# One large gate projection ahead of the level products, and a new order of work between the last mixer half and the first expert

## What is computed

```python
h = rmsnorm(x, g_pre_mix) * (1.0 + sc_mix) + sh_mix
proj = h @ w_in                                   # u | q k v | z | a | b
pool_out, _ = pool_mixer(u, pool_buf, start_pos, w_pool, pool_scale)
qkv_c, _ = causal_conv(qkv, conv_buf, conv_w)
o, s_new = gated_delta_rule(q, k, v, g, beta, s0)  # solves (I + L) T = I per chunk
o = o * rsqrt(mean(o * o) + EPS) * gdn_norm_w * silu(z)
x = x + gt_mix * rmsnorm(concat([pool_out, o]) @ w_out, g_post_mix)
h = rmsnorm(x, g_pre_ffn) * (1.0 + sc_ffn) + sh_ffn
logits = h @ router_w + router_b                  # 32 experts, top 4, softmax gates
f = sum over the 4 chosen experts e of gate_e * ((up_e + 1) * glu_e) @ w_down[e] + b_down[e]
x = x + gt_ffn * rmsnorm(f, g_post_ffn)
```

## Time and profile before

| | us |
|---|---|
| runs, median (lowest to highest, 3 runs) | 1219.59 (1217.38 to 1220.33) |
| the profiled execution's own time | 1221.47 |
| its span | 1219.5 |
| TensorE matmul busy | 1032.8 (85%) |
| VectorE busy | 396.7 (33%) |
| ScalarE busy | 168.6 (14%) |
| GpSimd busy | 125.7 (10%) |
| moved by DMA | 463.68 MB, 380 GB/s in the mean |

### The profile page before, as it was taken

The page is one execution under the profiler, slowest core; times in us unless marked ns, Lnnn a source line. Parts: engine busy times, 40 slices in busy tenths (PEclk is TensorE's granted clock), DMA queues, the critical chain, the costliest instruction groups (busy, mean ns, idle before and its releaser), DMA issues.

```text
span 1219.5 us, 31937 instructions
## 1 busy us (share of the span) xinstructions
PE 1032.8 (85%) x11996; PEld 503.7 (41%) x11997; DVE 396.7 (33%) x1155; ACT 168.6 (14%) x459; POOL 125.7 (10%) x325
## 2 busy tenths in 40 slices
PE   4899997997899869899779999898856799999864
PEld 4678775646333314333223334333311233334321
DVE  1044594765323213133113332332211223223313
ACT  2252313133000000010001001001000000001002
POOL 0042003100111001001101110100100000000100
PEclk9898998997999989999889999999988899999997
DMA  9945936989899999999999997999999999999996
GB/s 338 337 144 207 328 131 185 343 298 389 360 426 427 429 429 429 427 429 427 429 429 428 427 429 301 430 430 427 428 428 428 430 430 427 428 428 428 430 430 280
DMA packets 77831, 463.68 MB, mean 380 GB/s; under 512 B 11531, under 2 KB 31185, under 8 KB 53146
## 3 DMA queue, kind: packets, MB, share of 16 engines
q1 hardware_dynamic: 70479, 460.88, 92.1%
q10 hardware_dynamic: 7315, 2.27, 0.9%
HBM read 455.56 MB, written 7.57 MB: 380 GB/s over the span
## 4 chain that ended last, share of the span: by engine, by line
PE 62%; DMA 18%; DVE 9%; SPq 4%; issue 4%; ACT 1%; DVEq 1%; ACTq 0%; POOLq 0%; POOL 0%
PE psum L663 26%; PE psum L682 14%; DMA weights<-in_w_gu 11%; PE psum L638 4%; PE psum L1027 4%; DMA work<-in_w_down 4%; SPq L914 2%; PE psum L615 2%; PE psum L1278 2%; PE psum L632 2%; DMA weights<-in_w_ada 2%; PE psum L1032 1%; DVE work L2404 1%; DVE work L2048 1%; DVE work L2409 1%
## 5 line engine op out<-in xcount | busy, mean ns | idle before, releaser
L663 PE MATMUL psum<-weights,work 128*32 128x512 f32 x2928 | 346.6, 613 | 89.4 <-DMA weights<-in_w_gu 45.1
L663 PEld LDWEIGHTS psum<-weights,work 128*32 128x32 f32 x2928 | 92.8, 111 | 311.7 <-issue 240.2
L682 PE MATMUL psum<-weights,work 128*32 128x256 f32 x2624 | 162.3, 398 | 35.4 <-DVE work L2418 32.1
L2404 DVE STREAM_TRANSPOSE work<-psum 128x256 f32<-128x256 f32 x53 | 23.9, 450 | 425.8 <-PE psum L663 425.8
L682 PEld LDWEIGHTS psum<-weights,work 128*32 128x32 f32 x2624 | 84.5, 114 | 107.8 <-issue 58.3
L1824 ACT ACTIVATE work<-work x53 | 22.1, 416 | 505.6 <-DVE work L2408 505.6
L615 PE MATMUL psum<-work 128*32 128x257 f32 (+3 forms) x1296 | 88.9, 387 | 1.1 <-ACT work L1771 1.1
L2428 DVE STREAM_TRANSPOSE work<-work 128x288 f32<-128x288 f32 x53 | 25.3, 478 | 191.8 <-PE psum L638 191.8
L1027 PE MATMUL psum<-work,weights 128*128 128x288 f32 x320 | 81.0, 410 | 0.0
L663 PE MATMUL psum<-work 128*32 128x512 f32 x464 | 60.0, 637 | 8.9 <-DMA work<-in_w_gu 8.9
L1027 PEld LDWEIGHTS psum<-work,weights 128*128 128x128 f32 x320 | 59.8, 190 | 17.5 <-issue 1.8
(11 more groups left out here) (405 smaller groups left out, 933.6 us busy)
## 6 DMA issues: line engine op xcount, KB each, us to landing
weights<-in_w_gu SPq DMA_DIRECT2D x112, 2048.0 KB, 35.7
weights<-in_w_down SPq DMA_DIRECT2D x48, 2048.0 KB, 38.1
work<-in_w_gu SPq DMA_DIRECT2D x16, 2048.0 KB, 32.4
work<-in_w_down SPq DMA_DIRECT2D x16, 2048.0 KB, 42.6
weights<-in_w_ada SPq DMA_DIRECT2D x12, 2048.0 KB, 12.6
weights<-in_w_in SPq DMA_DIRECT2D x6, 2048.0 KB, 13.4
weights<-in_w_out SPq DMA_DIRECT2D x2, 2048.0 KB, 8.3
out<-weights SPq DMA_DIRECT2D x8, 512.0 KB, 10.1
```

The costliest lines, as they stand in the source:

```text
L663: last = mm(bank(GB)[SLOTS * n:SLOTS * n + SLOTS, :].rearrange("p (a x) -> p a x", a=4), xTm[:, k, :], gu[:, k % 2, n], start=k == 0, stop ...
L682: last = mm(bank(YB)[SLOTS * q:SLOTS * q + SLOTS, 0:QW], hT[:, k, :], dn[:, k % 4, QW * q:QW * q + QW], start=k == 0, stop=k == KT - 1)
L2404: v.transpose(features, of_slots[0]).then_inc(s["hid_step"], 1)
```

## The change

There are two parts. **In the front part** the work after unit 23 moves behind unit 24, and that after unit 24 behind unit 25, on TensorE and ScalarE alike; the last transposes of values come ahead of the last level's updates. On SP the eight small stores of modulated gates and the load of the sequence mask go ahead of the store of solved blocks; the sample states are loaded right behind the blocks, and the gate rows (`gate_rows`) after them.

**Between the last mixer half and the first expert** `normed` writes the whole scaled chunk, and TensorE transposes it with its transpose operation; the last state products stand inside the last mixer half (5 of its 8 matmuls, then the state, then 3); the third chunk is transposed and brought back ahead of other work; gates are normalized on VectorE ahead of the ranks, VectorE sets the first gate column in GpSimd's place, one gather takes all 257 columns after the gate's transposes, and the products with zeros are gone (the bias products start the accumulators). On SP the stores and loads of the second expert are reordered.

The core of the diff (ScalarE's units move as TensorE's do, its `rows_back` as TensorE's `back`; bank numbers are left out):

```diff
-        diag = [X3.at(2 * GW + P * c, P) for c in range(3)]
+        xt = [M.at(6400, D), M.at(3072, D), mix_s]
...
+                    if first and c == 2:
+                        pe.wait_ge(s["h2"], 3)
...
-            pe.wait_ge(s["h2"], 3)
-            pe.wait_ge(s["rank_done"], 2)
-            gather_by(sel_first, QW).then_inc(s["router_ps"], 1)
+                    mm(samples_out[r, :], gT[r, span(2)], b_down_sb[r, :], start=True, stop=False)
+
+            pe.wait_ge(s["h2"], 2)
+            pe.wait_ge(s["rank_done"], 1)
             for r in range(NQ):
                 for q in range(NQ):
                     rows, to = slice(SLOTS * r, SLOTS * r + SLOTS), slice(SLOTS * q, SLOTS * q + SLOTS)
-                    last = mm(bank(GB)[to, 2 * NE * r:2 * NE * (r + 1)], ident[:, rows], rank[:, 0:2, :].rearrange("p c e -> p (c e)"),
+                    last = mm(bank(RB)[to, 2 * NE * r:2 * NE * (r + 1)], ident[:, rows], rank[:, 0:2, :].rearrange("p c e -> p (c e)"),
                               start=True, stop=True)
             last.then_inc(s["router_ps"], 1)
-            pe.wait_ge(s["selT"], 1)
-            for half in range(2):
-                for q in range(NQ):
-                    r = slice(NE * q, NE * q + NE)
-                    mm(total(q, half), selT[r, 0:P], consts_sb[r, 0:QW], start=half == 0, stop=False)
-            mm(samples_out, selT[0:NE, 0:P], consts_sb[0:NE, 0:QW], start=True, stop=False)
-            pe.wait_ge(s["cum"], 4)
-            of_first = bounds(0)
             pe.wait_ge(s["gate_done"], 1)
             for c in range(3):
                 for q in range(NQ):
-                    last = mm(bank(YB)[NE * q:NE * q + NE, AT[c]:AT[c] + ROWS[c]], gate[0:ROWS[c], c, :],
+                    last = mm(bank(TB)[NE * q:NE * q + NE, AT[c]:AT[c] + ROWS[c]], gate[0:ROWS[c], c, :],
                               ident[0:ROWS[c], 0:ROWS[c]], start=True, stop=True)
             last.then_inc(s["router_ps"], 1)
+            pe.wait_ge(s["rank_done"], 2)
             pe.wait_ge(s["cur_set"], 2)
-            pe.wait_ge(s["xTm"], 1)
-            for c in range(3):
-                for g in range(NQ):
-                    r = slice(SLOTS * g, SLOTS * g + SLOTS)
-                    last = mm(bank(XB)[r, QW:GC], sel_first[r, c, :] if c == 2 else sel_first[:, c, :],
-                              h2s[r, QW:GC] if c == 2 else h2[:, c, g, QW:GC], start=c == 0, stop=c == 2)
-            last.then_inc(s["xg_ps"], 1)
-            pe.wait_ge(s["gbT"], 1)
-            pe.wait_ge(s["rank_b"], 1)
+            gather_by(sel_first, GC, True).then_inc(s["xg_ps"], 1)
+            pe.wait_ge(s["cum"], 4)
+            of_first = bounds(0)
             expert(0, 0, of_first)
             for r in range(1, PERIOD):
                 expert(0, r)
...
             sp.dma_start(w_out_sb[1], w_out_half(1)).then_inc(s["wout_in"], 16)
+            sp.wait_ge(s["modG"], 4)
+            for j in range(4):
+                sp.dma_start(gm_dram[:, :, P * j:P * j + P], modG[32 * j:32 * j + SEQS]).then_inc(s["side_st"], 16)
+            sp.wait_ge(s["slot_used"], used("in", 5))
+            sp.dma_start(seqmask, cc("seqmask").rearrange("p (b t) -> p b t", b=NSEQ)).then_inc(s["seq_in"], 16)
+            for j in range(4):
+                sp.dma_start(gs_dram[:, j // 2, :, j % 2].rearrange("t b c -> b t c"), modG[32 * j + 1:32 * j + SEQS, 2:4]
+                             ).then_inc(s["side_st"], 16)
             sp.wait_ge(s["pooled"], 2)
             sp.wait_ge(s["t0"], 2)
             sp.dma_start(t_dram.rearrange("c h r k i j -> (c h r) (k i j)"), blk_tu[0:BLOCKS]).then_inc(s["blk"], 16)
             t_block_loads(sp, 0)
-            sp.wait_ge(s["modG"], 4)
-            for j in range(4):
-                sp.dma_start(gm_dram[:, :, P * j:P * j + P], modG[32 * j:32 * j + SEQS]).then_inc(s["modG_st"], 16)
-            sp.wait_ge(s["slot_used"], used("in", 5))
-            sp.dma_start(seqmask, cc("seqmask").rearrange("p (b t) -> p b t", b=NSEQ)).then_inc(s["seq_in"], 16)
-            for j in range(4):
-                sp.dma_start(gs_dram[:, j // 2, :, j % 2].rearrange("t b c -> b t c"), modG[32 * j + 1:32 * j + SEQS, 2:4]
-                             ).then_inc(s["modG_st"], 16)
-            sp.wait_ge(s["modG_st"], 128)
-            gate_rows(sp, 0, gm_tok, "gm_in")
+            sp.wait_ge(s["side_st"], 128)
             sp.wait_ge(s["pool_ps"], 2)
             sp.wait_ge(s["s_silu"], 3)
             sp.wait_ge(s["norm_ps"], 2)
...
                 sp.dma_start(Ssm[:, :, b], state_ssm[0, b].rearrange("h k v -> k h v")).then_inc(s["ssm_in"], 16)
+            gate_rows(sp, 0, gm_tok, "gm_in")
...
             sp.wait_ge(s["mix_ps"], 3)
             load(1, 0)
             store_states(1)
+            store_states(2)
+            sp.wait_ge(s["mix_ps"], 4)
+            load(1, 1)
             sp.wait_ge(s["ssm_out"], 16 * 5)
             load(1, 2)
-            sp.wait_ge(s["mix_ps"], 4)
-            load(1, 1)
             for q in range(NQ):
                 sp.dma_start(bgu_rows[NE * q:NE * q + NE], b_gu[0].rearrange("e (a n x) -> n e a x", a=4, n=NQ)[q]
                              ).then_inc(s["bgu_in"], 16)
+            store_x1(2)
+            load(1, 4)
+            sp.wait_ge(s["x2T_ps"], 3)
             for q in range(NQ):
                 sp.dma_start(b_down_sb[NE * q:NE * q + NE, :], b_down[0][:, QW * q:QW * q + QW]).then_inc(s["rb_in"], 16)
-            store_states(2)
-            store_x1(2)
+            sp.wait_ge(s["side_st"], 128 + 32)
+            load(1, 3)
             sp.wait_ge(s["x2T_ps"], 5)
-            load(1, 4)
-            sp.wait_ge(s["ssm_out"], 16 * (1 + H))
-            load(1, 3)
...
-                if u == 23:
+                if u == 24:
                     pe.wait_ge(s["qkdT"], 3)
                     pe.wait_ge(s["blk"], 16 * BLK_LOADED)
                     level_product(pe, mm, 1)
                     conv_tails()
                     level_updates(pe, mm, 1)
                     level_updates(pe, mm, 2)
-                if u == 24:
+                if u == 25:
                     pe.wait_ge(s["kv_tok"], 4)
                     to_tokens(4, PB)
                     level_product(pe, mm, 3)
                     level_product(pe, mm, 4)
                     last_tails()
-                    level_updates(pe, mm, 3)
-                    level_updates(pe, mm, 4)
-                if u == 25:
                     pe.wait_ge(s["s_silu"], 3)
                     pe.wait_ge(s["kv_tok"], 5)
                     to_tokens(5, PB)
+                    level_updates(pe, mm, 3)
+                    level_updates(pe, mm, 4)
 
...
-                    last = mm(out, x_sb[0:n, c, P * k:P * k + P], diag[c][0:n, 0:n], start=True, stop=True)
+                    last = tr(out, xt[c][0:n, P * k:P * k + P], ident[0:n, 0:n])
...
             state_update(1, 1)
             pe.wait_ge(s["ssq"], 5)
             state_update(2, 0)
-            mix_half(1, 4, 1).then_inc(s["mix_ps"], 1)
+            mix_half(1, 4, 1, 0, 5)
+            state_update(2, 1)
+            mix_half(1, 4, 1, 5).then_inc(s["mix_ps"], 1)
             transposes_x2(0, 6)
-            state_update(2, 1)
-            pe.wait_ge(s["s_new"], 2 * H)
+            pe.wait_ge(s["s_new"], 2 * H - 2)
             transposes_x2(1, 1)
             logit_parts(0, 6, 7)
+            transposes_x2(2, 4)
+            logit_sums(0, 7)
             sample_logits(1)
-            logit_sums(0, 7)
-            transposes_x2(2, 4)
             pe.wait_ge(s["lg_sb"], 2)
             back(0, 6)
             pe.wait_ge(s["lg_sb"], 3)
+            pe.wait_ge(s["s_new"], 2 * H)
             logit_parts(2, 1, 2)
+            back(2, 4)
+            logit_sums(2, 2)
             earlier_ranks()
-            logit_sums(2, 2)
+            last_ranks()
             pe.wait_ge(s["h2"], 1)
             back(1, 6)
-            last_ranks()
-            back(2, 4)
-            pe.wait_ge(s["h2"], 2)
...
-                ts(diag[c][0:n, 0:n], ident[0:n, 0:n], st[0:n, 4 + c:5 + c], None, ALU.mult).then_inc(s["xn2"], 1)
+                ts(xt[c][0:n, :], x_sb[0:n, c, :], st[0:n, 4 + c:5 + c], None, ALU.mult).then_inc(s["xn2"], 1)
...
-            for t in range(2):
-                new_states(2, 0, t)
+            for m in range(2):
+                for t in range(2):
+                    new_states(2, m, t)
             add_mix(2)
-            for t in range(2):
-                new_states(2, 1, t)
             normed(2)
             v.wait_ge(s["x2T_ps"], 3)
             v.wait_ge(s["modT"], 4)
...
+            v.wait_ge(s["gate_done"], 1)
+            ts(gate_col[:, 0:2 * NQ].rearrange("p (c g) -> p c g", c=2), gate[:, 0:2, 0:1].to_broadcast([P, 2, NQ]),
+               1.0 / ALPHA, None, ALU.mult).then_inc(s["cur_set"], 1)
+            ts(gate_col[:, 2 * NQ:], gate[:, 2, 0:1], 1.0 / ALPHA, None, ALU.mult).then_inc(s["cur_set"], 1)
...
-            v.wait_ge(s["router_ps"], 7)
```

(14 more changed lines are left out.)

61 lines of the change are left out of this document (28 added, 33 removed).

## The result

The changed kernel takes 1211.47 us (median of 5 runs, 1205.39 to 1212.91), the kernel before 1218.16 us beside it (5 runs, 1217.38 to 1220.33): a ratio of 0.9925, with a 95% interval of 0.9905 to 0.9945. It is faster, as forecast, but by 6.7 us in place of 17.3, and outside the range of 1199.5 to 1208.5. The profiled execution took 1211.84 us (span 1210.1).

A forecast was written before the change was run, and what follows sets the result against it. The DMA stream of expert weights was taken as the bound, TensorE only around the dip at 738 to 754 us. Gains of 10.0 + 5.0 + 2.3 = 17.3 us gave 1219.59 - 17.3 = 1202.3 us, range 1199.5 to 1208.5.

The forecast's parts named there:

- (1): Before the level products: unit 24 fills TensorE's 7.16 us wait for solved blocks; gain 7.1 us.
- (3): Products from L1245 on no longer wait for a copy on ScalarE; gain 1.4 us.
- Term (4): Level products: unit 25 and six transposes cover VectorE and ScalarE putting results back; price 0, up to 1.5 us otherwise.
- Term (5): SP's front order: early small stores, sample states issued from about 188.3 us, and later gate rows all cost 0.
- Term (2): Level products: without idle time TensorE's clock stays at 2.4 GHz; gain 1.5 us, bounds 0 and 2.5.
- Term (6): Front: state loads closely following the last block pieces delay those pieces by 0, at most 1.9 us.
- Term (7): Before the first expert: an earlier first reload removes DMA's pause at 305 to 314 us; gain 5.0 us.
- Term (8): Router stretch: earlier stores of the last states fill DMA's idle time; gain 2.3 us, bounds 1 and 2.5.
- A: Last mixer half to first expert: TensorE at half clock, a DMA pause stays; 1203.3 to 1207.3 us, chance 0.14.
- B: Level products: steps wait for VectorE and ScalarE, or sample states come late; 1206.7 us, chance 0.14.
- C: Front: blocks land later, so the large projection does not fill the wait; 1210 to 1211 us, chance 0.05.
- D: TensorE-bound stretch up to 768 us: held at 1.2 GHz, the kernel gets slower; 1223.3 us with 42 us, chance 0.02.

The follow-up runs named there:

- e11: Changed kernel with sample states loaded head by head: two heads behind the block pieces, four behind the last projection unit, then gate rows; 1206.35 us, ratio 0.9888.
- e7: Changed kernel with gate rows issued first, then all sample states head by head behind the last projection unit; 1206.41 us, ratio 0.9888.
- e8: Changed kernel with products by a scaled diagonal in place of VectorE's scaling and TensorE's transposes; 1210.84 us, ratio 0.9916.
- e1: Kernel before with only the front part of the change; 1214.07 us, ratio 0.9972.
- e12: Kernel before with only the front part, states by head: two behind the block pieces, four behind the last projection unit; 1209.35 us, ratio 0.9934.
- e2: Changed kernel without the front part of the change; 1213.86 us, ratio 0.9958.
- e3: Changed kernel, but SP waits for the last projection unit before issuing the eight state loads; 1213.10 us, ratio 0.9961.

## Why the prediction was right and wrong

**The bound** was read rightly. From 314 us on the stream of DMA runs at 428 GB/s in every trace, and its lead at 100 MB is kept up to the dip: against the second trace of before it is 4.9 us in the changed kernel at 100 MB and 4.8 at 240 MB, and 11.6 and 11.5 in e11.

**Terms (1) and (3)** held: no wait for the blocks (7.16 us before), none in front of L1245's successor (1.38 before). **Term (4)** held at 0.

**Term (5) is the step that failed.** It let the states' loads start earlier "as far as the products that need them" and priced them at 0. Nothing in that sentence asks what else is on DMA at that moment. **Term (2)** held where it was read and was undone by the stop: from the first level products to the next unit TensorE needs 3.1 us (189.38 - 186.28) in place of 5.0, 1.9 won for 1.5 reckoned, but behind the stop more was lost again at 1.2 GHz. The price is the difference of the stretches in the changed kernel and e11, 52.9 - 45.4 = 7.5 us: 3.0 for the stop (3.54 less 0.58), and 4.5 for the work behind it, from the transposes to the first products for the states (11.3 us in place of 6.8). Without it (e11) the stretch is 8.7 to 9.8 us shorter than in the two traces of before, where the prediction had 10.0. In the time, by the ratios of the runs, the stop costs 4.5 us: e11 is 1206.35 us, 13.6 us below before by its ratio, so with the stop gone the sum of 17.3 is still 3.7 too high.

**Term (6)** looked at the right collision and the wrong victim. By the Trainium skill's rule on turns between queues (DMA: Bandwidth & Descriptors, "Queues, rings and completion order") I asked only what the states do to the block pieces, bound 1.9 us. They did nothing to them (no wait at 186.28), but the states' packets held up the fetch of instructions: it starts 19.5 us behind the large projection in the changed kernel and 17.0 in e7. The Trainium skill (Runtime: NRT & Kernel Launch, "Instruction fetch mechanics") says that the fetch goes through a DMA queue in blocks of 16 KiB, which the packets above bear out, and that the cost of crossing a block boundary is mostly hidden; here it is not, by 2.5 to 3.9 us in six kernels.

**Part two's lead** of 11 us (bounds 7 and 13) measured 12.9 and 13.7 us against the two traces of before, but not by its terms. The transposes, counted at 4 us, gave 0.6 to 1.4 (e8): right on the engine, wrong on the path, since waits took the rest. The 6.1 us between the gather's end and the expert came true (0.5 us in place of 6.5 in the second trace of before). Part of what made up for the transposes is the clock, which I had left at 0.7: it was 0.86 at 275 to 285 us and 1.00 at 285 to 295, where the second trace of before has 0.67 in both; the gather took 1.6 us in place of 2.9. The rest of the sum was not taken apart. That the lead came out above 11 is luck, and so is the expert's place: 286.99 is near the 286 that was foretold, because 3.7 us of faster front in this execution and 2.7 us more of lead stand in for most of what part one lacked.

**Term (7)** was nearly right, but the pause differs between executions: from the position of 80 MB in the stream to that of 100 MB it took 51.7 and 51.0 us in the two traces of before, and 47.0 after, which is 4.7 and 4.0 us for the 5.0 reckoned; in e1 and e12, which still have the pause, it took 49.9 and 50.2. **Term (8)** was too high, and in the changed kernel it cannot be seen at all. DMA's share at 262 to 275 rose to 0.99 as said. From 60 to 80 MB the stream takes 60.1 and 59.6 us in the two traces of before and 58.4 in e2, and without the stop 54.3 in e12 and 53.0 in e11: part two gives 1.2 to 1.7 us there, not 2.3. In the changed kernel the same 20 MB take 61.1 us, since DMA's idle time at 235 to 245 went from 3.1 us (5 x 0.37 + 5 x 0.24) to 4.3 (5 x 0.76 + 5 x 0.09). There the loads wait for TensorE, which had not come forward; in e11 and e12, where it has its lead, the share at 235 to 245 is 0.98 to 1.06.

**The rivals.** A did not occur; 1 us of lead more or less did not matter, as e8 shows. Of B the clause "the sample states come late" is half of what happened, with the sign turned: they came too early. C named about the right time, 1210 to 1211, by luck, for another reason (the projection did fill the wait). D occurred in small: the last wait for DMA ahead of the stretch in which TensorE is the bound sometimes ends with 16 products at half clock.

```profile
616.17 3.33 PE L665 MATMUL psum<-weights,work 128*32 128x512 f32 x16 [2.13 <-DMA weights<-in_w_gu]
...
620.94 1.92 PE L663 MATMUL psum<-weights,work 128*32 128x512 f32 x16 [1.32 <-DMA weights<-in_w_gu]
```

The first row is of the changed kernel, the second of the second trace of before. Where they take 1.92 us (both traces of before, e3, e11, e12) the stream needs 102.1 to 102.5 us from 240 to 280 MB, where they take 2.84 to 3.59 us (the other nine) 103.2 to 104.4. The changed kernel lost 1.4 us so. Whether the edit has part in it or it is chance of the execution is open: e3 and e11, on the changed kernel's program, do not have it.

**The sum** by the two nearest traces: 4.8 us at the stream, less 1.4 in that stretch, is 3.4 (the spans, 1213.8 and 1210.1, differ by 3.7); by the medians it is 6.7. The execution of the second trace of before was 3.3 us below the median beside it (1215.79 and 1219.09), so the traces give the shares and the medians the size. I had put all weight on one trace of before that was 1.9 us above its median in total and 4 us in its front.

## What to carry to other kernels

Before a step is called free because it is only issued earlier, list everything that moves by DMA at its new time, the instructions themselves included: 3 MB of states, moved at some 300 GB/s, in front of the fetch stopped an engine that waited for no semaphore. (The stop came in a run of short products; that these use the fetched instructions up faster is likely, but was not tried.) An "issue" wait of microseconds with a full DMA and an instruction packet in it is the sign; the remedy is to issue that traffic in pieces, each just in time for its reader. And take a second trace of before: positions differed by 4 us between two executions here, and the same stretch by 1.2 (by 3.2 with e2, whose program is the same there).

## What the hardware showed that I had not expected

A stop of TensorE of 2.5 to 3.9 us for want of instructions in six kernels, 0.5 to 1.0 us in five, decided by when 3 MB of states are issued. The clock more than doubles the price of such a stop: after 3.5 us of standing still the granted clock was 0.50 to 0.58 for 10 us, and the work there took 4.5 us more. The stretch with the transposes did not have a lower clock than the same stretch with products (0.85 in both, though the Trainium skill, TensorE: Matmul & The Clock Gate, "Part 4: PE-mode transpose", has transposes not counted as busy). That is a weak test of the page, since the transposes are only 3.6 of its 23 us. And two executions of one kernel differed by 4 us in their first 176 us.
